# A two-block transformer kernel: the attention pairs' copies, waits and fill order moved

## The reference

```python
proj = rms_norm(x) @ w_in[l]
sb_q, sb_k, sb_v, sw_q, sw_k, sw_v, gate_logits = split(proj)   # 8 heads of 64; sw_k, sw_v: 2 heads
# stick-breaking branch, per head, keys s < t
z = q k^T * d**-0.5
w[t,s] = exp(log_sigmoid(z[t,s]) - sum_{s<j<t} softplus(z[t,j]));  o_sb = w @ v
# local branch: rope(rms_norm(q)), rope(rms_norm(k)), window of 128 keys, a sink in the softmax
p = softmax([scores, sink])[..., :-1];  o_swa = p @ v
x = x + (g0 * (o_sb @ w_branch_sb) + g1 * (o_swa @ w_branch_swa)) @ w_out
x = x + relu(rms_norm(x) @ w_up)**2 @ w_down
```

## Time and profile before

| | |
|---|---|
| median of 3 runs | 2807.17 us (2807.05 to 2807.38) |
| profiled execution | 2806.42 us, span of its trace 2805.0 us |
| mean granted PE clock | 0.997 |
| PE busy | 2728.8 us, 97% |
| DVE / ACT / POOL busy | 1516.5 / 1163.1 / 114.5 us |
| memory read | 231.57 MB, 83 GB/s over the span |

### The profile page before, as it was taken

The page is one execution under the profiler, slowest core; times in us unless marked ns, Lnnn a source line. Parts: engine busy times, 40 slices in busy tenths (PEclk is TensorE's granted clock), DMA queues, the critical chain, the costliest instruction groups (busy, mean ns, idle before and its releaser), DMA issues.

```text
span 2805.0 us, 30657 instructions
## 1 busy us (share of the span) xinstructions
PE 2728.8 (97%) x12366; PEld 2190.4 (78%) x12366; DVE 1516.5 (54%) x2093; ACT 1163.1 (41%) x1734; POOL 114.5 (4%) x79
## 2 busy tenths in 40 slices
PE   8999999999999999999999999999999899999998
PEld 6778778888887888887666888888876668888887
DVE  5566657565687747476444454443554445544433
ACT  6444344243475424254454333322345543333322
POOL 2333110000010000000000000000000000000000
PEclk9999999999999999999999999999999999999999
DMA  5111112223323322232111222222221112222322
GB/s 176 46 62 52 49 59 99 98 90 105 105 98 100 102 97 98 98 106 77 43 45 38 87 96 96 98 98 98 98 68 42 42 46 90 98 91 90 104 98 75
DMA packets 66955, 235.64 MB, mean 84 GB/s; under 512 B 7552, under 2 KB 8320, under 8 KB 66816
## 3 DMA queue, kind: packets, MB, share of 16 engines
q1 hardware_dynamic: 63504, 228.58, 24.6%
q10 hardware_dynamic: 3312, 5.12, 0.6%
HBM read 231.57 MB, written 2.10 MB: 83 GB/s over the span
## 4 chain that ended last, share of the span: by engine, by line
PE 84%; ACT 7%; DVE 5%; issue 2%; POOL 1%; DMA 0%; ACTq 0%; SPq 0%; DVEq 0%
PE bank L408 25%; PE bank L410 25%; PE bank L409 25%; ACT w_hi_k L892 1%; PE bank L762 1%; ACT p_t_att L1297 1%; PE bank L822 1%; PE bank L751 1%; PE bank L802 1%; DVE w_lo_k L1386 1%; PE bank L558 1%; ACT e_t_att L1261 1%; POOL q_mix L1982 1%; ACT e_t_att L1263 1%; POOL v_mix L1982 1%
## 5 line engine op out<-in xcount | busy, mean ns | idle before, releaser
L408 PE MATMUL bank<-x_hi_k,w_hi_k 128*128 128x512 f32 x2152 | 873.7, 406 | 13.0 <-DVE x_lo_k L1393 11.9
L892 ACT ACTIVATE w_hi_k<-raw_k 128x1024 fp32r<-128x1024 f32 x431 | 454.4, 1058 | 951.0 <-PE bank L410 948.9
L410 PE MATMUL bank<-x_hi_k,w_lo_k 128*128 128x512 f32 x2152 | 843.0, 392 | 0.0
L409 PE MATMUL bank<-x_lo_k,w_hi_k 128*128 128x512 f32 x2152 | 841.8, 391 | 0.0
L1386 DVE TENSOR_TENSOR w_lo_k<-raw_k,w_hi_k 128x1024 fp32r<-128x1024 f32 x431 | 532.8, 1236 | 175.6 <-ACT w_hi_k L892 175.6
L408 PEld LDWEIGHTS bank<-x_hi_k,w_hi_k 128*128 128x128 f32 x2152 | 406.3, 189 | 113.9 <-issue 16.9
L410 PEld LDWEIGHTS bank<-x_hi_k,w_lo_k 128*128 128x128 f32 x2152 | 405.9, 189 | 86.8
L409 PEld LDWEIGHTS bank<-x_lo_k,w_hi_k 128*128 128x128 f32 x2152 | 406.8, 189 | 83.8 <-issue 4.1
L408 PE MATMUL bank<-y_hi_k,w_hi_k 128*128 128x512 f32 x1136 | 445.5, 392 | 3.1 <-DVE y_lo_k L1714 1.8
L410 PE MATMUL bank<-y_hi_k,w_lo_k 128*128 128x512 f32 x1136 | 442.8, 390 | 0.0
L409 PE MATMUL bank<-y_lo_k,w_hi_k 128*128 128x512 f32 x1136 | 442.8, 390 | 0.0
(11 more groups left out here) (316 smaller groups left out, 2517.5 us busy)
## 6 DMA issues: line engine op xcount, KB each, us to landing
raw_k<-wstream SPq DMA_DIRECT2D x431, 512.0 KB, 3.2
outT<-h_k ACTq DMA_DIRECT2D x8, 256.0 KB, 2.9
h_k<-xT SPq DMA_DIRECT2D x4, 256.0 KB, 8.4
h_k<-xT ACTq DMA_DIRECT2D x4, 256.0 KB, 7.7
decay_mix<-constants ACTq DMA_DIRECT2D x4, 256.0 KB, 2.7
levels_mix<-constants SPq DMA_DIRECT2D x1, 448.0 KB, 11.1
vec_k<-vectors SPq DMA_DIRECT2D x1, 282.5 KB, 9.8
cos_mix<-constants SPq DMA_DIRECT2D x1, 256.0 KB, 10.2
```

The costliest lines, as they stand in the source:

```text
L408: pe.matmul(dst, wh, rh, start=start, stop=False)
L409: pe.matmul(dst, wh, rl, start=False, stop=False)
L410: return pe.matmul(dst, wl, rh, start=False, stop=stop)
L892: act.activation(k.w_hi[:, u % SPLIT, :], k.raw[:, u % RAW, :], ACT.Copy).then_inc(*hi_done.mark())
```

## The change

Five edits. First, the copies of stick queries and keys (`queries_and_keys`) are made on DVE at the end of the pair before, after the last "sums", instead of at the pair's own start; the first pair of a layer makes them where it did. Second, the window has one more empty step in each half between the transposes and the local output, so 25 steps, and they are placed up to 0.95 of the pair. Third, the first pair of a layer projects its local queries first (`FIRST_PAIR`), in the same banks by turn, so that its stick values are the last unit. Fourth, ACT squares the local queries of a layer's first pair right after the local keys' root, and waits for the local keys before that pair's own root. Fifth, in the first feed-forward wave of layer 0 a third unit is run four tiles behind.

```diff
+FIRST_PAIR = (3, 0, 1, 2)
...
-        units += [("pair", layer, 0, n) for n in range(4)]
+        units += [("pair", layer, 0, n) for n in FIRST_PAIR]
...
-        BANK["pair", _layer, 0, _n] = (2, 3, 4, 1)[_n]
+        BANK["pair", _layer, 0, _n] = (3, 4, 1, 2)[_n]
...
-WINDOW_STEPS = 6 + 2 * 8 + 1
+WINDOW_STEPS = 6 + 2 * 9 + 1
...
-    return ((stick, STICK_STEPS, 0, 1), (window, WINDOW_STEPS, 0, 0.9),
+    return ((stick, STICK_STEPS, 0, 1), (window, WINDOW_STEPS, 0, 0.95),
...
-    def wave_by_tile(names, xh, xl, event, made, lag, between=None):
+    def wave_by_tile(names, xh, xl, event, made, lags, between=None):
+        begun, rest = names[:len(lags)], names[len(lags):]
         for kk in range(KT):
             pe.wait_ge(*dve_done.at(*made(kk)))
-            blocks(UNIT[first], BANK[first], [kk], xh, xl, KT)
-            if kk >= lag:
-                blocks(UNIT[second], BANK[second], [kk - lag], xh, xl, KT)
+            for name, lag in zip(begun, lags):
+                if kk >= lag:
+                    blocks(UNIT[name], BANK[name], [kk - lag], xh, xl, KT)
...
-                wave_by_tile(ups, k.x_hi, k.x_lo, "pad", x_made(stage), 2,
+                wave_by_tile(ups, k.x_hi, k.x_lo, "pad", x_made(stage), (0, 2, 4),
...
             mm.then_inc(*mark("pT", *at, half))          # PE, window
             yield
+            yield
             pe.wait_ge(*act_done.at("pT", *at, half))
...
     def window(layer, m):                                 # ACT
         at = (layer, m)
+        yield
         if m == 0:
-            window_squares(layer, 0)
-        yield
+            act.wait_ge(*dve_done.at("wk", layer))
...
         inverse_root(k.rstd[:], bank[6][:], 1.0 / 64, "wk_root", layer)   # ACT, attention
+        window_squares(layer, 0)
         first.rest()
...
+    def queries_and_keys(layer, pair):                    # DVE
         at = (layer, pair)
+        dve.wait_ge(*dve_done.at("fill", UNIT["pair", layer, pair, 1]))
         dve.tensor_copy(k.aq[:], k.lands[0][:]).then_inc(*mark())
         for half in range(2):
             r, other = head_rows(half)
             mm = dve.tensor_copy(k.zk[r, half, :], k.lands[1][r, :])
             mm.then_inc(*(mark("qk", *at) if half else mark()))
+
+    def stick(layer, pair):
+        at = (layer, pair)
+        if pair == 0:
+            queries_and_keys(layer, 0)
         yield
...
+            if n == 2 * TC and pair < 3:
+                queries_and_keys(layer, pair + 1)
             yield
```

More of the change, by code:

```diff
@@ L441, in wave @@
             project(name, xh, xl, event, K)
-    def wave_by_tile(names, xh, xl, event, made, lag, between=None):
-        first, second = names[:2]
+    def wave_by_tile(names, xh, xl, event, made, lags, between=None):
+        begun, rest = names[:len(lags)], names[len(lags):]
         for kk in range(KT):
             pe.wait_ge(*dve_done.at(*made(kk)))
-            blocks(UNIT[first], BANK[first], [kk], xh, xl, KT)
-            if kk >= lag:
-                blocks(UNIT[second], BANK[second], [kk - lag], xh, xl, KT)
+            for name, lag in zip(begun, lags):
+                if kk >= lag:
+                    blocks(UNIT[name], BANK[name], [kk - lag], xh, xl, KT)
         if between:
             between()
-        if lag:
-            blocks(UNIT[second], BANK[second], range(KT - lag, KT), xh, xl, KT)
-        for name in (first, second):
+        for name, lag in zip(begun, lags):
+            if lag:
+                blocks(UNIT[name], BANK[name], range(KT - lag, KT), xh, xl, KT)
             emptied[BANK[name]] = (dve_done, (event, UNIT[name]))
-        for name in names[2:]:
+        for name in rest:
             project(name, xh, xl, event)
@@ L716, in pe_program @@
         project(("lru_gate", m), k.x_hi, k.x_lo, "lru_g")
-    wave_by_tile([("lru_out", m) for m in range(KT)], k.y_hi, k.y_lo, "added", lambda kk: ("lru_y", kk), 0)
+    wave_by_tile([("lru_out", m) for m in range(KT)], k.y_hi, k.y_lo, "added", lambda kk: ("lru_y", kk), (0, 0))
     conv_ffn(1)
@@ L830, in attention @@
              between=(lambda: sum_squares(bank[7][:], k.ssum, stage)) if layer == 1 else final_sums)
-        first = Fill([("pair", layer, 0, n) for n in range(4)], fill_piece)
+        first = Fill([("pair", layer, 0, n) for n in FIRST_PAIR], fill_piece)
         first.part(4)
@@ L1784, in h_final @@
                                      ALU.mult).then_inc(*mark("h_final"))
-    def stick(layer, pair):
+    def queries_and_keys(layer, pair):
         at = (layer, pair)
+        dve.wait_ge(*dve_done.at("fill", UNIT["pair", layer, pair, 1]))
         dve.tensor_copy(k.aq[:], k.lands[0][:]).then_inc(*mark())
@@ L1885, in fill_piece @@
             w_low()
-        first = Fill([("kv", layer, n) for n in range(2)] + [("pair", layer, 0, n) for n in range(4)], fill_piece)
+        first = Fill([("kv", layer, n) for n in range(2)] + [("pair", layer, 0, n) for n in FIRST_PAIR], fill_piece)
         first.part(8)
```

1 line of the change is left out of this document (added).

## The result

The changed kernel takes 2784.51 us (median of 4 executions, 2783.30 to 2784.81) where the one before takes 2807.14: a ratio of 0.9919, with a 95% interval of 0.9907 to 0.9932. The forecast was 2784.5. The time is met almost to the last digit, but that is in part luck: the gains were worked out about 4 us too small, and so was the loss, and the two errors cancel.

A forecast was written before the change was run, and what follows sets the result against it. TensorE was taken as the bound, busy 2728.8 of 2805.0 us, so at most 76 us of waits could go. 8.0 + 18.0 + 1.4 - 4.7 = 22.7 us gave 2784.5 us, range 2778 to 2790.

The forecast's parts named there:

- The start of the six pairs: Pairs 2 to 4 of each layer: z0 no longer waits for copies, scores come 1.34 us sooner, 8.0 us in six.
- The clock: Behind the scores' pause: slow stretches (partly 1.2 instead of 2.4 GHz) in three of six pairs, 4.7 us given back.
- The second half: Of each pair: lw6's wait for sums and the local output's for `pT` go, 0.77 + 1.48 us, 18.0 us in eight.
- The feared wait at the transposes: Second half: transposes wait for probabilities late behind the fill; 1.1 us x 8 comes back, 2793 us; chance 0.04.
- rival of the second half: Late probabilities, 2793 us (0.04); the same much larger, 2813 us (0.02); waits only change place, 2805 to 2810 us (0.03).
- The first pairs: First pair of each layer: z0 and the scores stay in place; 0 us, ends -0.5 and +0.5 for both layers.
- The wave: Feed-forward wave, fifth to eighth tiles: a third unit's tiles fill TensorE's waits, 1.4 us, ends 0 and 2.1.
- first rival: Behind the scores: no slow stretches, or one; all 27.4 us stay, 2779.8 us; chance 0.15.
- Its second: Pair starts: slow stretches in five or six pairs, 2787.6 to 2789.2 us, or little gain there, 2792.5 us; chance 0.15.
- a slow stretch in every pair: Sign against the forecast: the lower clock behind the pause in every pair, where two to four slow stretches were forecast.

The follow-up runs named there:

- Copies alone: The kernel before with only the copies of stick queries and keys moved to the end of the pair before: 2801.32 us against 2806.86, ratio 0.9980.
- undone: The changed kernel with the copies put back at the start of their own pair: 2784.43 us, ratio 0.9919.
- undone with the pause covered: The changed kernel with one more empty window step ahead of the scores and the copies back at their own pair's start: 2771.02 us, ratio 0.9871.

## Why the prediction came out

**The start of the six pairs: right in its mechanism, a little small.** The forecast had the scores at 8.88 us behind the sum of squares; it is 8.82. It moved them by 1.34 us in each pair. Measured, it is 1.40, and 1.76 in layer 0's second pair, whose scores had stood at 10.57, since the slow stretch there was not swallowed whole. That is 8.8 us instead of 8.0. The wait at the scores was forecast as "some 2.5 us" and is 2.54. Copies alone, undone and undone with the pause covered all agree that the local queries' chain was next.

**The clock: right in its mechanism, wrong in its count.** The step that failed is "I take the odds of before, three of the six later starts: 3 x 1.56 = 4.7 us given back". The profile has six stretches and 9.1 us. The odds themselves can't be read from one trace. The same 2.54 us pause brought two of six, three of six and six of six in different programs, and between executions of one program the time moved by 6 us. That a stretch is due to the pause is shown: it moves with it, behind z0 where z0 waits and behind the scores where they wait, and with the pause at 0.44 us or less there is none in the pairs of two kernels. What chooses the pairs in which it comes stays open; it hangs on more than the pause's length. The second mixer layer has one more case, which no edit touches. TensorE waits 1.85 us for `y_lo` there in every kernel. In eight of the thirteen profiles, before and after among them, the clock falls behind it, and in five it doesn't. With the copies alone it did not, and a second wait of 1.40 us follows:

```profile
867.35 0.50 PE L408 MATMUL bank<-y_hi_k,w_hi_k 128*128 128x512 f32 x1 [1.85 <-DVE y_lo_k L1714]
...
871.76 0.50 PE L408 MATMUL bank<-y_hi_k,w_hi_k 128*128 128x512 f32 x1 [1.40 <-DVE y_lo_k L1714]
```

The windows behind the 1.85 us in that kernel and in the one before:

```profile
867.30:871.30 4.00, 3.02 (x12) 2.17 (x12) 3.90 (x6) 2.83 (x4) 0.00 (x0) 1.00 0.14 46
866.50:870.50 4.00, 3.98 (x11) 3.17 (x12) 3.90 (x6) 2.83 (x4) 0.00 (x0) 0.62 0.19 41
```

Where the clock falls, the second wait is gone and nothing is lost: from the wave's third tile to the first pair it is 907.64 us before and 907.66 with the copies alone.

The Trainium skill, page "TensorE: Matmul & The Clock Gate", section "HAM oscillation — how this bites in real kernels", would have had no loss behind pauses as short as these. The measurement decides against it: 4.78 to 5.03 us instead of 3.41 from the scores to z2.

**The second half: right, mis-sized.** 0.77 + 1.48 = 2.25 us a pair was forecast. The runs show 2.60 (52.14 less 49.54), 20.8 us in eight instead of 18.0. From F14 to lw6 it is now 1.48 us where it was 2.24, and from the transposes to what follows 0.79 where it was 2.34: 2.31 us of it. The rest is in the products behind, which follow closer when no wait stands ahead of them, such as 1.56 instead of 1.66 us for the local output. The 0.17 us added to the bracket were right for lw6 and too little for the local output (1.55 us in place of 1.48), and the products behind were left out. The feared wait at the transposes did not come: DVE's probabilities were done at 1468.47 and the transposes began at 1469.72, a cover of 1.25 us where 1.4 was worked out. No rival of the second half came.

**The first pairs: right.** Nothing, alone and in the whole.

**The wave: right, somewhat small.** 1.7 to 2.0 us by the traces instead of 1.4.

**The sum.** 8.8 + 20.8 + 2.0 - 9.1 = 22.5 us against 22.7 forecast and 22.6 measured. The two profiled executions lie 22.0 us apart; the wave's third tile, ahead of everything that the edits touch, comes 0.5 us later in the one after. The gains were 4.2 us larger than worked out and the loss 4.4 us larger. The forecast's first rival, no slow stretches, was wrong here. Its second, the stretches in five or six pairs (2787.6 to 2789.2 us), is what happened, and the larger gains hid it in the time. The forecast named a slow stretch in every pair as a sign against itself; it came in each of the six whose copies were moved. A time that agrees says little of its terms: the waits, windows and the kernels with one part alone were needed to see this.

## What to carry to other kernels

When a wait is taken from the front of a chain, work out what ends last behind it before counting the gain: here taking away the copies' 2.29 us in six pairs was worth 5.5 us alone, nothing in the changed kernel, and 14.7 us once the next chain was covered. A pause moved to a place where no later wait swallows its after-effects can cost the engine's clock as well as its time. And in a hand-woven order, first try how much work stands in front of each wait; one figure, 0.9 to 0.95, gave more than the five edits together.

## What the runs showed of the hardware

In the attention pairs TensorE's granted clock fell behind pauses of 1.88, 2.29 and 2.54 us, in some pairs and not in others (in two of six at 1.88 us, in none to four of six at 2.29, in two to six of six at 2.54), and behind one of 1.85 us elsewhere in eight of thirteen profiles. It never fell behind those of 1.37 to 1.40 us, or behind two of 0.8 and 1.28 us close together; in the kernel before it also fell once behind 1.29 and 0.73 us in a row. One fall costs 1.4 to 1.7 us where no later wait swallows it. The number of falls can change the time of one program by 6 us from execution to execution, so a difference of a few us between two kernels with such pauses says little until the falls are counted. Back-to-back small fp32 products overlap more than their durations show: eight transposes that last 1.04 us let the next product start after 0.79.
